# One ScalarE copy moved behind the second exponential in the attention stage of a fused two-block kernel

## The chip, the cores and the metric

The kernel runs on one core of a Trainium2 chip. A core has engines that run their own instruction queues and meet through semaphores: TensorE (PE, matrix products), VectorE (DVE), ScalarE (ACT), GpSimd (POOL) and SyncE (SP, which mostly issues DMAs). Products land in PSUM, eight banks of 512 fp32 columns on 128 partitions; ScalarE and VectorE read them from there. The metric is the device time of one execution in microseconds (us).

## The reference

The program computes two transformer-like blocks, one after the other, on 1024 tokens of width 1024. The first has differential attention, retention and a mixture of 32 experts, the second a gated convolution and an MLP. Only the differential attention matters here: four heads, each with two maps, causal in chunks of 64 tokens:

```python
s = jnp.einsum('bqhmd,bkhmd->bhmqk', q_blk, k) * scale
s = jnp.where(allowed, s + bias, -jnp.inf)
p = jax.nn.softmax(s, axis=-1)
a = p[:, :, 0] - lam * p[:, :, 1]
return jnp.einsum('bhqk,bkhe->bqhe', a.astype(v.dtype), v)
```

So every block of 128 queries needs the scores of two maps (m = 0 and 1), the softmax of each, their weighted difference, and the product with the values.

## The kernel before, in words

The kernel is written out by hand: each engine has one function with its instructions in order, and semaphores tie the functions together. No scheduler changes that order. The stages run one after the other: norm and transposes, the input projection (with retention in its middle), attention, output projection, router and experts, convolution, MLP.

The attention stage works on 32 blocks, numbered b. A block is one head h and one query tile i. Within each head the tiles come in the order 7, 0, 6, 1, 5, 2, 4, 3 (line 495), so that a large and a small block alternate. A block has i + 1 key tiles ("k tiles") of 128 columns, its width W is 128 times that. Even b are the large ones (8, 7, 6, 5 k tiles), odd b the small ones (1, 2, 3, 4). For each block:

- TensorE computes the scores of map m into SC(m), which is two PSUM banks of the tensor `ps` (lines 1815 to 1820). There is one such place for each map, so the scores of block b + 1 wait until the exponential of block b has read it (`att_exp`).
- VectorE takes the negated row maximum (line 1441, `att_max`).
- ScalarE takes the exponential with the row sum (line 1140, `att_exp`); the row sum leaves as a separate instruction, ACTIVATION_READ_ACCUMULATOR. The result goes to one of three buffers for each map, `PB`.
- VectorE, once both maps of the block have their sums, forms the reciprocals and the weighted difference (lines 1447 to 1453, `att_mixed`).
- TensorE transposes the difference, one k tile at a time, into two PSUM banks of `pt` (line 1830, `att_transposed`). There is a single place for this result.
- ScalarE copies the first four k tiles from there to SBUF (line 1122, `t_evac`, `att_t_act`), VectorE the k tiles above four, where there are any (line 1461, `late_evac`, `att_t_dve`). The next block's transposes wait for both.
- TensorE multiplies with the values (line 1844, `att_out`), and ScalarE reads the product twice, scaled and squared (lines 1127 and 1129, `o_evac`).

These steps are spread over several turns of the loop. In turn b TensorE issues: scores (b, 0), transposes (b - 2), scores (b, 1), output product (b - 3). VectorE issues: row maximum (b, 0), difference (b - 1), row maximum (b, 1), upper copy (b - 2). ScalarE issues: exponential (b, 0), copy (b - 2), exponential (b, 1), output readers (b - 3). The last turns, where no new scores exist, do what is left.

No DMA is issued inside the stage. GpSimd splits two weight units into halves at the stage's start (lines 982 and 984, up to 357 us).

Of the kernel before, what the change touches and what calls it, by code (L numbers as in the profile page):

```python
# [106 lines left out]
def build(nc, a, out):  # L107
    with ExitStack() as ctx:
# [122 lines left out]
        def tpair(par):  # L231
            return PT[:, 2 * par:2 * par + 2, :].rearrange("p b (k c) -> p (b k) c", k=4)
# [263 lines left out]
        NB = len(BLOCKS)  # L496

        def aT(par):
            return XTF[:, 6144 + par * 1024:6144 + (par + 1) * 1024].rearrange("p (k q) -> p k q", k=KT)

        def PB(b, m):
            i = 2 * (b % 3) + m
            return XTF[:, i * 1024:i * 1024 + 1024]

        def SC(m):
            return PS[:, 2 * m:2 * m + 2, :].rearrange("p b c -> p (b c)")
# [554 lines left out]
        def _(act):  # L1061
# [54 lines left out]
            def t_evac(b):  # L1116
                par = b % 2
                act.wait_ge(s_at, b + 1)
                if b >= 2:
                    act.wait_ge(s_ao, b - 1)  # L1120
                n = min(4, BLOCKS[b][1] + 1)
                nc.scalar.activation(aT(par)[:, 0:n, :], tpair(0)[:, 0:n, :], ACT.Copy).then_inc(s_aea, 1)

            def o_evac(b):
                h, i = BLOCKS[b]
                act.wait_ge(s_ao, b + 1)
                nc.scalar.activation(H[:, i, h * DV:(h + 1) * DV], PT[:, 2 + b % 2, 0:DV], ACT.Copy,
                                     scale=rows_rec[:, 2 * b:2 * b + 1])
                nc.scalar.activation(Z[:, b % 8 * DV:b % 8 * DV + DV], PT[:, 2 + b % 2, 0:DV],
                                     ACT.Square, scale=rows_rec[:, 2 * b:2 * b + 1],  # L1130
                                     accum_out=ssA[:, h * TT + i:h * TT + i + 1]).then_inc(s_aoe, 1)

            for b in range(NB + 3):
                if b < NB:
                    W = P * (BLOCKS[b][1] + 1)
                    for m in range(2):
                        act.wait_ge(s_amx, 2 * b + m + 1)
                        if b >= 3:
                            act.wait_ge(s_at, b - 2)
                        nc.scalar.activation(PB(b, m)[:, 0:W], SC(m)[:, 0:W], ACT.Exp,  # L1140
                                             bias=negmax[:, 2 * b + m:2 * b + m + 1],
                                             accum_out=rows_sum[:, 2 * b + m:2 * b + m + 1]).then_inc(s_ae, 1)
                        if m == 0 and b >= 2:
                            t_evac(b - 2)
                if NB <= b < NB + 2:
                    t_evac(b - 2)
                if b >= 3:
                    o_evac(b - 3)
# [1018 lines left out]
```

## Time and profile before

| | us |
|---|---|
| three executions | 2341.51, 2339.02, 2333.03 |
| median | 2339.02 |
| profiled execution, device time | 2341.51 |
| its span, first to last instruction | 2339.8 |
| TensorE busy | 2128.6 (91%) |
| VectorE busy | 1234.3 (53%) |
| ScalarE busy | 906.5 (39%) |
| GpSimd busy | 199.1 (9%) |

The attention lies between about 336 and 468 us of the span. From the second head on a head lasts 29.7 us: its first row maximum begins at 374.25, 403.99 and 433.74 us. A profile row in order of time gives the start, the duration, the engine, the line, what is written and read, and, in brackets, how long the engine stood idle before it and which instruction released it. Idle time counts only where the engine is on the path that sets the end. The granted clock is the share of full speed that TensorE's throttle allowed. Durations of neighbouring rows overlap where an engine is pipelined, so the distance of two starts says how long the engine is taken.

### The profile page before, as it was taken

The page shows a single profiled execution, that of the slowest core. Times are in us where ns is not written, and L with a number is a line of the kernel's source. Part 1 is how long each engine was busy: PE and PEld are TensorE (multiplying, and loading weights), DVE is VectorE, ACT ScalarE, POOL GpSimd, SP SyncE. Part 2 cuts the span into 40 slices and gives each one's busy share as a digit, 9 for nine tenths or more (in the row PEclk, how much of TensorE's full clock was granted, in tenths as well). Part 3 has the DMA queues.
Part 4 walks back from the last instruction along what each step waited for, and adds up shares of the span by engine and source line. Part 5 has one row for each costly group of instructions (what it writes and reads, how often), then busy time and mean ns, then how long its engine had stood idle before and what let it go on. Part 6 is the DMA issues. An engine that isn't in the chain of part 4 may idle for free.

```text
span 2339.8 us, 28085 instructions
## 1 busy us (share of the span) xinstructions
PE 2128.6 (91%) x10811; PEld 1091.7 (47%) x10811; DVE 1234.3 (53%) x1374; ACT 906.5 (39%) x1219; POOL 199.1 (9%) x264
## 2 busy tenths in 40 slices
PE   5998988888399999999945899959999999999999
PEld 3445446644244445445423465544444444444444
DVE  4225237744688888888867152384534343343432
ACT  4122126722267666666744152372312112211210
POOL 1000031000111111111120010022000000000000
PEclk9999999999699999999977899979999999999999
DMA  9101220051399999999975043325201011010001
GB/s 380 56 37 37 63 54 1 1 210 55 111 416 422 422 412 417 417 413 417 408 266 225 28 153 113 98 85 180 73 36 72 36 56 52 36 72 36 36 0 72
DMA packets 77020, 378.62 MB, mean 162 GB/s; under 512 B 12368, under 2 KB 19152, under 8 KB 44368
## 3 DMA queue, kind: packets, MB, share of 16 engines
q1 hardware_dynamic: 54000, 296.82, 32.1%
q0 software_dynamic: 22944, 80.75, 9.7%
q8 instruction: 52, 0.85, 0.2%
q14 instruction: 24, 0.20, 0.0%
HBM read 326.67 MB, written 37.75 MB: 156 GB/s over the span
## 4 chain that ended last, share of the span: by engine, by line
PE 86%; DVE 7%; issue 3%; DMA 2%; ACT 1%; SPq 1%; POOL 1%; POOLq 0%; DVEq 0%; ACTq 0%
PE ps L409 22%; PE ps L411 22%; PE ps L410 22%; PE pt L1954 5%; PE pt L409 1%; PE pt L410 1%; PE pt L411 1%; PE pt L1908 1%; DVE cols L1441 1%; PE pt L463 1%; PE pt L1844 1%; PE pt L2010 1%; PE pt L2012 1%; PE pt L2011 1%; DMA resid<-in_x 1%
## 5 line engine op out<-in xcount | busy, mean ns | idle before, releaser
L409 PE MATMUL ps<-xt,split 128*128 128x512 f16 x960 | 370.3, 386 | 22.8 <-issue 13.8
L409 PE MATMUL ps<-split,xt 128*128 128x512 f16 x928 | 354.5, 382 | 25.5 <-DMA xt<-arena 20.0
L410 PE MATMUL ps<-xt,split 128*128 128x512 f16 x960 | 369.7, 385 | 0.0
L411 PE MATMUL ps<-xt,split 128*128 128x512 f16 x960 | 369.4, 385 | 0.0
L411 PE MATMUL ps<-split,xt 128*128 128x512 f16 x928 | 354.4, 382 | 0.0
L410 PE MATMUL ps<-split,xt 128*128 128x512 f16 x928 | 354.3, 382 | 0.0
L546 DVE SCALAR_TENSOR_TENSOR split<-stage,split 128x2048 f16<-128x2048 f32 x128 | 290.1, 2287 | 57.8 <-ACT split L542 57.8
L542 ACT ACTIVATE split<-stage 128x2048 f16<-128x2048 f32 x128 | 237.1, 1901 | 121.1 <-PE ps L411 121.1
L411 PE MATMUL ps<-split,arena 128*128 128x512 f16 x512 | 194.3, 379 | 0.0
L410 PE MATMUL ps<-split,arena 128*128 128x512 f16 x512 | 194.3, 379 | 0.0
L409 PE MATMUL ps<-split,arena 128*128 128x512 f16 x512 | 194.3, 379 | 0.0
L1723 DVE SCALAR_TENSOR_TENSOR resid<-ps,resid 128x512 f32<-128x512 f32 x128 | 87.2, 690 | 191.7 <-PE ps L411 191.6
L409 PEld LDWEIGHTS ps<-xt,split 128*128 128x128 f16 x960 | 95.0, 99 | 139.0 <-issue 27.0
L1708 DVE TENSOR_TENSOR arena<-arena 128x512 f32<-128x512 f32 x64 | 44.3, 692 | 218.6 <-ACT arena L1322 218.6
L669 ACT ACTIVATE split<-stage 128x2048 f16<-128x2048 f32 x32 | 59.4, 1900 | 252.9 <-PE ps L411 252.9
L409 PEld LDWEIGHTS ps<-split,xt 128*128 128x128 f16 x928 | 91.3, 98 | 135.8 <-issue 35.2
L411 PEld LDWEIGHTS ps<-xt,split 128*128 128x128 f16 x960 | 95.2, 99 | 117.2 <-issue 6.9
L410 PEld LDWEIGHTS ps<-xt,split 128*128 128x128 f16 x960 | 95.1, 99 | 114.7 <-issue 5.5
L410 PEld LDWEIGHTS ps<-split,xt 128*128 128x128 f16 x928 | 91.2, 98 | 112.5 <-issue 12.5
L411 PEld LDWEIGHTS ps<-split,xt 128*128 128x128 f16 x928 | 91.2, 98 | 111.0 <-issue 2.7
L1322 ACT ACTIVATE arena<-ps 128x512 f32<-128x512 f32 x64 | 38.2, 597 | 244.1 <-PE ps L411 244.1
L1954 PE MATMUL pt<-arena,xt 128*128 128x512 f32 x256 | 115.1, 593 | 0.0
(291 smaller groups left out, 3010.3 us busy)
## 6 DMA issues: line engine op xcount, KB each, us to landing
stage<-in_w_gate SPq DMA_DIRECT2D x64, 1024.0 KB, 7.9
stage<-in_w_up SPq DMA_DIRECT2D x64, 1024.0 KB, 8.0
arena<-in_w_down SPq DMA_DIRECT2D x64, 1024.0 KB, 9.9
stage<-in_w_mlp SPq DMA_DIRECT2D x32, 1024.0 KB, 5.3
y_rows<-arena POOLq DMA_DIRECT2D x48, 512.0 KB, 8.7
arena<-in_conv_taps POOLq DMA_DIRECT2D x32, 576.0 KB, 4.3
stage<-in_w_dense_a SPq DMA_DIRECT2D x16, 1024.0 KB, 8.9
stage<-in_w_dense_b SPq DMA_DIRECT2D x12, 1024.0 KB, 9.0
```

Of the source, the lines that this page charges most:

```text
L409: nc.tensor.matmul(out_ap, lh, rh, start=start, stop=False)
L410: nc.tensor.matmul(out_ap, lh, rl, start=False, stop=False)
L411: return nc.tensor.matmul(out_ap, ll, rh, start=False, stop=stop)
L463: i = nc.tensor.transpose(tpair(t % 2)[:, k, :], src(t, k), ident)
L542: nc.scalar.activation(whi(s), wstage(s), ACT.Copy, scale=WS).then_inc(s_wh[s], 1)
L546: nc.vector.scalar_tensor_tensor(out=wlo(s), in0=wstage(s), scalar=WS, in1=whi(s), op0=ALU.mult, op1=ALU.subtract).then_inc(s_wo[s], 1)
L669: nc.scalar.activation(whi(s), wstage(s), ACT.Copy, scale=WS).then_inc(s_wh[s], 1)
L1322: nc.scalar.activation(relu[j % 2], PS[:, j % 4, :], ACT.Relu, scale=IWS)\
L1441: nc.vector.tensor_reduce(negmax[:, 2 * b + m:2 * b + m + 1], SC(m)[:, 0:W], AX.X, ALU.max, negate=True).then_inc(s_amx, 1)
L1708: nc.vector.tensor_tensor(relu2[j % 2], relu[j % 2], relu[j % 2], ALU.mult).then_inc(s_relu, 1)
L1723: nc.vector.scalar_tensor_tensor(out=H[:, t, hs], in0=PS[:, j % 4, :], scalar=IWS, in1=H[:, t, hs], op0=ALU.mult, op1=ALU.add).then_inc(s_ ...
L1954: m = nc.tensor.matmul(PT[:, 3, :], hTf[:, k, :], native(q)[:, k * UC:k * UC + UC], start=k == 0, stop=k == UK - 1)
```

## The change

In ScalarE's loop the copy of block b - 2 stands between the two exponentials of block b before the change. After it, the copy stands behind both, ahead of the output readers of block b - 3. The copy, its waits and its signal are the same, and so are all other instructions. In the last turns (b = 32, 33) nothing changes place.

```diff
@@ -1140,9 +1140,7 @@
                         nc.scalar.activation(PB(b, m)[:, 0:W], SC(m)[:, 0:W], ACT.Exp,
                                              bias=negmax[:, 2 * b + m:2 * b + m + 1],
                                              accum_out=rows_sum[:, 2 * b + m:2 * b + m + 1]).then_inc(s_ae, 1)
-                        if m == 0 and b >= 2:
-                            t_evac(b - 2)
-                if NB <= b < NB + 2:
+                if 2 <= b < NB + 2:
                     t_evac(b - 2)
                 if b >= 3:
                     o_evac(b - 3)
```

Place one, ScalarE at the start of a head (turns b = 24 and 25, the large block with 8 k tiles and the small one with 1). Before, `L1140` is the exponential, `L1122` the copy, `L1127` and `L1129` the output readers; `att_transposed` is given by the transposes, `att_max` by the row maximum:

```order
L1140 ACTIVATE xt,cols<-ps,cols 128x1024 [waits att_transposed,att_max]
L1122 ACTIVATE xt<-pt 128x512 [waits att_out,att_transposed]
L1140 ACTIVATE xt,cols<-ps,cols 128x1024 [waits att_transposed,att_max]
L1127 ACTIVATE resid<-pt,cols 128x128 [waits att_out]
L1129 ACTIVATE zone,cols<-pt,cols 128x128
L1140 ACTIVATE xt,cols<-ps,cols 128x128 [waits att_transposed,att_max]
L1122 ACTIVATE xt<-pt 128x512 [waits att_out,att_transposed]
L1140 ACTIVATE xt,cols<-ps,cols 128x128 [waits att_transposed,att_max]
```

The same place in the changed kernel, where x2 are the two exponentials in a row:

```order
L1140 ACTIVATE xt,cols<-ps,cols 128x1024 [waits att_transposed,att_max] x2
L1122 ACTIVATE xt<-pt 128x512 [waits att_out,att_transposed]
L1127 ACTIVATE resid<-pt,cols 128x128 [waits att_out]
L1129 ACTIVATE zone,cols<-pt,cols 128x128
L1140 ACTIVATE xt,cols<-ps,cols 128x128 [waits att_transposed,att_max] x2
L1122 ACTIVATE xt<-pt 128x512 [waits att_out,att_transposed]
```

The copy of block 22 has moved behind the second exponential of block 24, and the copy of block 23 behind the second exponential of block 25.

Place two, TensorE at the turn that follows (turn 25 begins with the first row; this order is the same before and after). `L1815` to `L1820` are scores, `L1830` transposes, `L1844` the output product; `att_t_act` is given by ScalarE's copy, `att_t_dve` by VectorE's:

```order
L1815 MATMUL ps<-arena 128x128 [waits att_exp]
L1816 MATMUL ps<-xn,arena 128x128
L1817 MATMUL ps<-zone 128x128
L1820 MATMUL ps<-half 128x128
L1830 MATMUL pt<-misc,xt 128x128 [waits att_t_dve,att_t_act,att_mixed]
L1830 MATMUL pt<-misc,xt 128x128 x3
L1815 MATMUL ps<-arena 128x128 [waits att_exp]
```

Nothing moved here: the transposes of block 23 wait for the copy of block 22, and the second scores of block 25 stand behind them.

Place three, ScalarE at the end of the stage (turn b = 31 and what follows). Before:

```order
L1140 ACTIVATE xt,cols<-ps,cols 128x512 [waits att_transposed,att_max]
L1122 ACTIVATE xt<-pt 128x384 [waits att_out,att_transposed]
L1140 ACTIVATE xt,cols<-ps,cols 128x512 [waits att_transposed,att_max]
L1127 ACTIVATE resid<-pt,cols 128x128 [waits att_out]
L1129 ACTIVATE zone,cols<-pt,cols 128x128
```

And in the changed kernel:

```order
L1140 ACTIVATE xt,cols<-ps,cols 128x512 [waits att_transposed,att_max] x2
L1122 ACTIVATE xt<-pt 128x384 [waits att_out,att_transposed]
L1127 ACTIVATE resid<-pt,cols 128x128 [waits att_out]
L1129 ACTIVATE zone,cols<-pt,cols 128x128
```

The last copy that moves is that of block 29; those of blocks 30 and 31 stand where they stood.

## Rows read from the trace of the kernel before

**Rows 1.** The page: the chain that ended last, by engine.
```profile
PE 86%; DVE 7%; issue 3%; DMA 2%; ACT 1%; SPq 1%; POOL 1%; POOLq 0%; DVEq 0%; ACTq 0%
```

**Rows 2.** Stretches: busy us (x instructions) of PE, PEld, DVE, ACT, POOL; clock, DMA.
```profile
404.00:433.70 29.70, 26.68 (x198) 19.53 (x197) 22.42 (x44) 20.97 (x64) 0.00 (x0) 1.00 0.00 1
```

**Rows 3.** Waits from 353 to 462 us: who waited for whom, us, times, longest.
```profile
ACT xt L1140 <- DVE cols L1441: 36.3, 44, 4.3
...
DVE cols L1441 <- PE ps L1820: 19.2, 17, 1.7
DVE cols L1447 <- ACT xt L1140: 3.6, 7, 0.9
...
PE pt L1830 <- DVE xt L1461: 10.9, 15, 2.4
```

**Rows 4.** Order in time, ScalarE: start us, duration us, instruction, turn 24.
```profile
436.11 0.59 ACT L1122 ACTIVATE xt<-pt 128x512 f32<-128x512 f32 x1
437.30 1.11 ACT L1140 ACTIVATE xt<-ps,cols 128x1024 f32<-128x1024 f32 x1 [0.61 <-DVE cols L1441]
438.31 0.19 ACT L1140 ACTIVATION_READ_ACCUMULATOR xt<-ps,cols 128x1 f32 x1
438.41 0.36 ACT L1127 ACTIVATE resid<-pt,cols 128x128 f32<-128x128 f32 x1
```

**Rows 5.** Order in time, TensorE, turns 25 and 26.
```profile
437.61 0.63 PE L1830 MATMUL pt<-misc,xt 128*128 128x128 f32 x4 [0.95 <-DVE xt L1461]
438.56 0.23 PE L1815 MATMUL ps<-arena 128*128 128x128 f16 x1 [0.32 <-ACT xt L1140]
...
439.97 0.38 PE L1815 MATMUL ps<-arena 128*128 128x512 f16 x1
...
441.16 1.04 PE L1830 MATMUL pt<-misc,xt 128*128 128x128 f32 x8
442.04 0.38 PE L1815 MATMUL ps<-arena 128*128 128x512 f16 x1
```

**Rows 6.** Order in time, ScalarE turn 18 (7 k tiles), TensorE turn 19.
```profile
414.81 1.01 ACT L1140 ACTIVATE xt<-ps,cols 128x896 f32<-128x896 f32 x1 [0.49 <-DVE cols L1441]
...
415.52 0.30 PE L1830 MATMUL pt<-misc,xt 128*128 128x128 f32 x1 [0.54 <-DVE xt L1461]
415.96 0.28 PE L1815 MATMUL ps<-arena 128*128 128x256 f16 x1
```

**Rows 7.** Order in time, ScalarE turn 20 (6 k tiles), TensorE turn 21.
```profile
422.22 0.90 ACT L1140 ACTIVATE xt<-ps,cols 128x768 f32<-128x768 f32 x1 [0.33 <-DVE cols L1441]
...
422.80 0.41 PE L1830 MATMUL pt<-misc,xt 128*128 128x128 f32 x2 [0.61 <-DVE xt L1461]
423.27 0.34 PE L1815 MATMUL ps<-arena 128*128 128x384 f16 x1
```

**Rows 8.** Order in time, turns 22 (5 k tiles) and 23, three engines.
```profile
429.14 0.79 ACT L1140 ACTIVATE xt<-ps,cols 128x640 f32<-128x640 f32 x1 [0.40 <-DVE cols L1441]
...
429.58 0.52 PE L1830 MATMUL pt<-misc,xt 128*128 128x128 f32 x3 [0.38 <-DVE xt L1461]
430.08 0.39 PE L1815 MATMUL ps<-arena 128*128 128x512 f16 x1
...
431.37 0.68 DVE L1441 TENSOR_REDUCE cols<-ps 128x1 f32<-128x512 f32 x1
```

**Rows 9.** Order in time, VectorE, turns 25 and 26.
```profile
440.25 0.28 DVE L1441 TENSOR_REDUCE cols<-ps 128x1 f32<-128x128 f32 x1
441.36 1.09 DVE L1441 TENSOR_REDUCE cols<-ps 128x1 f32<-128x896 f32 x1 [0.82 <-PE ps L1820]
```

**Rows 10.** Stretches of TensorE alone: busy us (x), granted clock, DMA.
```profile
350.75:353.19 2.44, 0.00 (x0) 0.91 0.00 0
353.19:359.69 6.50, 6.50 (x28) 0.51 0.00 0
415.52:419.23 3.71, 3.57 (x29) 1.00 0.00 0
```

## The prediction, made before the changed kernel ran

> **What bounds the kernel now.** I read four views in this order. The page's chain of waits first: TensorE carries 86% of it, so time spent elsewhere counts only where TensorE stands still for it [rows 1]. Then the busy times of one head of the attention, the only stage that the change touches: in 29.7 us TensorE is busy 26.7, VectorE 22.4 and ScalarE 21.0 [rows 2]. ScalarE, whose order changes, is the least loaded of the three. Then the waits of the stage: ScalarE waits 44 times, 36.3 us in all, and always for VectorE's row maximum; VectorE waits 17 times, 19.2 us, for TensorE's scores; TensorE waits 15 times, 10.9 us, and that before the transposes, for the copy of the upper k tiles on VectorE (line 1461) [rows 3]. Last the order in time around such a wait.
>
> Names: S(b,m) are the score products of block b and map m, R(b,m) its row maximum (VectorE), E(b,m) its exponential (ScalarE), X(b) the transposes, T(b) ScalarE's copy of the first four k tiles out of PSUM, L(b) VectorE's copy of the others, A(b) the output products, O(b) their two readers on ScalarE. In step b TensorE runs S(b,0), X(b-2), S(b,1), A(b-3).
>
> **What the change takes away.** T(b-2) no longer stands ahead of E(b,1). It is 0.59 us for 512 columns. At each place shown it had ended before E(b,1) could begin: T(22) runs from 436.11 to 436.70 and E(24,1) then still waits 0.61 us for R(24,1), up to 437.30 [rows 4]. Of the 44 waits in rows 3, 30 stand before second maps, one before each from b = 2 on; the smallest at the places priced below is 0.33 us, at the third. So E(b,1) begins when it did, and the gain of the moved copy is 0. All of T was cover for a wait that remains.
>
> **What it adds.** X(b-1), one step later, writes the PSUM banks that T(b-2) reads and so waits for T(b-2) and L(b-2). Before, T was done long ahead and L, which starts right behind R(b,1), ended the wait. Now T starts only when E(b,1) is through, and E(b,1) itself starts after R(b,1). L is at most as long as T, so T is the later one wherever X is reached early. That is in every second step, where S(b+1,0) belongs to a small block (1 to 4 k tiles) and is over soon. In the other steps X comes behind the scores of five to eight k tiles, and the copy (behind a short exponential) is ready.
>
> Two lags are read off. The next ScalarE instruction starts where the duration of an exponential ends (437.30 + 1.11 = 438.41), and TensorE starts 0.06 us after the accumulator read behind an exponential ends (438.31 + 0.19 = 438.50, start at 438.56) [rows 4, 5]. Thus X can start at E's start + E's duration + 0.59 + 0.06. Eight transposes take from 441.16 to 442.04, 0.11 each [rows 5]. S(b+1,1) follows X, and had waited until then for E(b,1) [rows 5], so only the part of the delay beyond that wait is a loss:
> - Place 1, after 8 k tiles: X at 438.41 + 0.65 = 439.06 where it was at 437.61; four transposes, S at 439.52 where it was at 438.56: 0.96 us [rows 4, 5].
> - Place 2, after 7 tiles: X at 414.81 + 1.01 + 0.65 = 416.47 (was 415.52), one transpose, S at 416.58 (was 415.96): 0.62 [rows 6].
> - Place 3, after 6 tiles: 422.22 + 0.90 + 0.65 = 423.77 (was 422.80), two, S at 423.99 (was 423.27): 0.72 [rows 7].
> - Place 4, after 5 tiles: 429.14 + 0.79 + 0.65 = 430.58 (was 429.58), three, S at 430.91 (was 430.08): 0.83 [rows 8].
>
> Does that reach the end? At place 1 S(25,1) ends near 439.52 + 0.42 = 439.94, while R(25,1) begins only at 440.25, because VectorE is in the subtraction of block 24 [rows 9]: the second map of the small block loses nothing. But A(22) stands directly behind S(25,1) in TensorE's queue, S(26,0) directly behind A(22), and R(26,0) begins at 441.36 when TensorE, not VectorE, is ready (0.82 us of wait) [rows 5, 9]. So the loss goes through TensorE's own queue into the next large block, and from there into everything. It is the same at the other three: VectorE's 17 waits in rows 3 stand there. Queued behind the later T on ScalarE are O(b-3) and E(b+1,0), both by at most 0.5 us; E(25,0) started at about 438.41 + 0.6, now at 439.5, and is over by 440.0, while S(26,0), which waits for it, starts only at 439.97 + 0.96 [rows 5]. No term from that. DMA: none is issued in the stage.
>
> Sum over four heads. Place 1 exists three times (it needs the head before): 2.9. Place 2 four times: 2.5; in the first head VectorE is slow there, and I take the same. Place 3 four times: 2.9. Place 4 three times: 2.5, and at the last one there is no next large block; what remains is the last E, 0.45 us later (S ends at 430.91 + 0.91 = 431.82 where R began at 431.37) [rows 8]: 0.5. Together **11.3 us**.
>
> **The clock.** At place 1 TensorE now stands still from 436.66 to 439.06, 2.40 us, where it was 0.95 [rows 5]. The trace has one such gap in this stage, 2.44 us, and the granted clock fell from full (2.4 GHz) to half (1.2 GHz) inside it (mean 0.91) and stayed there for the 6.5 us that followed. The same work (one transpose, scores, eight output tiles, scores) took 3.71 us later at full clock: 2.8 us lost [rows 10]. Bounds for each of the three gaps at place 1: 0 and 2.8. At the other places the gap is 1.4 to 1.6 us, for which no row shows a fall; I take 0. I take one fall of the three and, as a part of it may end earlier or lie on slack, 2.0 us. [...]
>
> Forecast: 11.3 + 2.0 = **13.3 us longer**. The profiled execution took 2341.51 us (span 2339.8); it would take 2354.8. That execution is the slowest of three, 2.5 above the median of 2339.02, so for a median I say **2352.3 us**.
>
> **Rivals**
> - A, the copies come late, no clock fall: 2339.0 + 11.3 = 2350.3. For it: the clock is at full in the whole head of rows 2. Against: the gap of rows 10.
> - B, a fall at all three gaps: 2339.0 + 11.3 + 8.4 = 2358.7. For it: each gap is as long as the one that fell. Against: that one came soon after another low stretch.
> - C, half is absorbed: the step behind a loss has waits of its own (VectorE before the subtraction 7 times, 3.6 us in all [rows 3]), and each place gives back about half: 2344.7. Against: the queue TensorE, R, TensorE has no such wait at the four places.
> - D, nothing: X is in fact held by L and the accumulator, and the copy comes no later than L: 2339. It needs R(b,1) to end over 1.4 us ahead of what the rows show.
> - E, faster: the waits of E(b,1) are put down to R but are partly T's. Then each of the 30 exponentials behind a copy starts up to 0.5 us earlier, the subtraction and S(b+1,1) with it. In the 15 large steps this would be up to 7 us: 2332. It decides from the point where T ends after R(b,1). Rows 4 and 6 to 8 show R ending 0.3 to 0.6 us after it, so I give it little.
>
> **How the numbers follow.** Forecast 0.42, A 0.26, B 0.15, C 0.08, D 0.05, E 0.04. No change means within 0.5%, which is 11.7 us, about what a measurement of this kernel can tell. The border lies inside my cases: of the forecast four fifths lie above it, of A two fifths, B all. Slower 0.34 + 0.10 + 0.15 = 0.59; faster 0.04; the same 0.37. Range: from C's 2344 to 2361, B with the 2.5 us by which medians differ. The likeliest one's own is 2349 to 2356.
>
> **What the profile will show.** If right: the wait of TensorE before the transposes is put down to ScalarE's copy (line 1122, which moves up two lines), about 15 times and some 25 us in all; heads last 32.5 to 33 us where they lasted 29.7, or 35 with a fall; ScalarE's waits for R keep their places; work after the attention is as long as before. Wrong: if transposes still wait for line 1461, if a head lasts under 31 us, or if TensorE's granted clock is below full at every head. If E(b,1) starts earlier against R(b,0) than before, case E holds.

## The result and the profile after

The changed kernel took 2352.27 us (median of 6 runs, 2349.26 to 2354.6), the kernel before 2337.23 us (median of 6, 2333.03 to 2341.51). The ratio is 1.006 with a 95% interval of 1.0048 to 1.0073, that is 11 to 17 us: slower, clear of noise, though the lower end of the interval lies just under the 0.5% that I had called the border. The medians are 15.0 us apart; 13.3 was predicted.

The profiled execution took 2348.84 us (span 2347.1), where 2354.8 was forecast; that is 7.3 more than that of before. The two profiles differ outside the stage too, by 5.9 us in the other direction: ScalarE's first exponential begins 2.5 us earlier (337.75 against 340.22), and what follows the stage is 3.5 us shorter (1868.7 against 1872.15). Nothing was changed there, and the six runs of the kernel before spread by 8.5 us. So I judge by the stage itself, from ScalarE's first exponential to the table load behind the attention. It lasted 127.4 us before (340.22 to 467.65) and 140.6 after: 13.2 more.

The ends of the stage after, in order of time on ScalarE (start, duration, line):

```profile
337.75 1.11 ACT L1140 ACTIVATE xt<-ps,cols 128x1024 f32<-128x1024 f32 x1
...
478.40 1.28 ACT L1148 ACT_TABLE_LOAD   x1
```

Lines below the change have moved up by two: the transposes are now 1828, VectorE's row maximum 1439, its copy 1459. ScalarE's copy stands above the change and is still line 1122. The waits of the stage after (353 to 477 us; us in all, times, longest):

```profile
ACT xt L1140 <- DVE cols L1439: 44.3, 43, 4.0
DVE cols L1439 <- PE ps L1818: 31.2, 22, 2.8
...
PE pt L1828 <- ACT xt L1122: 24.0, 14, 2.4
```

Against [rows 3]: the transposes wait for ScalarE's copy where they waited for VectorE's, 24.0 us instead of 10.9, and no wait for VectorE's copy is left. That the 13.1 us between them are so near to the 13.2 that the stage grew is chance: over the whole stage the two are 26.5 and 11.8, the short waits before the second scores (0.32 us at 438.56 in [rows 5]) are gone, and a fall of the clock, below, is no wait. VectorE's wait for the scores grew by 12.0: the delay handed on.

The same place as [rows 4, 5, 9], in turns 24 to 26 after, engine by engine in order of time:

```profile
444.81 1.11 ACT L1140 ACTIVATE xt<-ps,cols 128x1024 f32<-128x1024 f32 x1 [1.10 <-DVE cols L1439]
445.91 0.59 ACT L1122 ACTIVATE xt<-pt 128x512 f32<-128x512 f32 x1
...
446.60 0.63 PE L1828 MATMUL pt<-misc,xt 128*128 128x128 f32 x4 [2.44 <-ACT xt L1122]
447.06 0.22 PE L1813 MATMUL ps<-arena 128*128 128x128 f16 x1
...
448.46 0.38 PE L1813 MATMUL ps<-arena 128*128 128x512 f16 x1
...
449.85 1.09 DVE L1439 TENSOR_REDUCE cols<-ps 128x1 f32<-128x896 f32 x1 [1.81 <-PE ps L1818]
```

The second exponential now waits 1.10 us for the row maximum, 0.61 + 0.49: the copy's whole place has turned into waiting. The copy ends at 446.50, the transposes start at 446.60, and the scores of the next large block (448.46) stand 1.40 us behind the second scores (447.06) of the small one, as before (438.56 to 439.97, 1.41).

The heads, from the first exponential of the large block to that of the next head (columns: length, busy time and count of TensorE, its weight loads, DVE, ACT and POOL, then the granted clock and the DMA's):

```profile
375.06:408.10 33.04, 26.06 (x198) 19.75 (x197) 22.61 (x45) 21.22 (x65) 0.00 (x0) 1.00 0.01 1
408.10:442.50 34.40, 27.42 (x198) 21.05 (x197) 22.70 (x45) 21.32 (x64) 0.00 (x0) 0.95 0.00 1
```

A head was 29.7 us [rows 2]. One head is now at full clock and 3.30 us longer, one has a fall of the clock and is 4.65 us longer. The gap at place 1 is 2.44 us in the second, the third and the fourth head alike, and the clock is not: it fell through that of the third head (the first two rows) and not through that of the fourth (TensorE alone: busy, granted clock):

```profile
409.75:412.19 2.44, 0.00 (x1) 0.89 0.00 0
412.19:416.09 3.90, 3.90 (x22) 0.63 0.00 0
444.16:446.60 2.44, 0.00 (x1) 1.00 0.01 3
446.60:450.50 3.90, 3.90 (x33) 1.00 0.02 4
```

In the same 3.90 us TensorE began 22 instructions at the lower clock and 33 at the full one.

### The profile page after: what moved, and what is told of

It is laid out like the page before. It is cut to its first block, busy times and chain, and to the rows that moved or that the text cites. A ratio compares the mean times of both kernels' runs of the same rounds, so it can differ in the third digit from the quotient of the medians.

```text
span 2347.1 us, 28085 instructions
## 1 busy us (share of the span) xinstructions
PE 2123.1 (90%) x10811; PEld 1092.8 (47%) x10811; DVE 1235.2 (53%) x1374; ACT 908.0 (39%) x1219; POOL 199.7 (9%) x264
## 4 chain that ended last, share of the span: by engine, by line
PE 84%; DVE 6%; issue 3%; SPq 3%; DMA 2%; ACT 1%; POOL 0%; POOLq 0%; ACTq 0%; DVEq 0%
PE ps L409 22%; PE ps L410 22%; PE ps L411 22%; PE pt L1952 5%; SPq L637 2%; PE pt L1906 1%; PE pt L409 1%; PE pt L411 1%; PE pt L410 1%; DVE cols L1439 1%; PE pt L463 1%; PE pt L1842 1%; PE pt L2008 1%; PE pt L2009 1%; PE pt L2010 1%
```

## The experiments

Each is measured by its heads (29.7 us before, 33.0 after at full clock) and its stage (127.4 and 140.6). First heads vary by a microsecond or two between executions, with the low clock at the stage's start, so a single stage length is good to about that; heads two and three repeat to 0.02 us where the clock is the same. Where a kernel has one timed execution, no ratio is given. The time in a head in which TensorE is not busy (its length less TensorE's busy time) is a second measure: it leaves out what a fall of the clock costs. In the changed kernel it is 33.04 - 26.06 = 6.98 us, at full clock and, within 0.01, with a fall.

**The copy between the exponentials in even turns alone.**

```diff
-                        if m == 0 and b >= 2:
+                        if m == 0 and b >= 2 and b % 2 == 0:
                             t_evac(b - 2)
-                if NB <= b < NB + 2:
+                if NB <= b < NB + 2 or (2 <= b < NB and not (b % 2 == 0)):
```

> The copy goes back between the two exponentials in the even turns (large blocks) alone; in odd turns it stays behind. Stage length is counted from ScalarE's first exponential to the table load behind the stage: 127.4 us before, 140.6 after the change. Theory (the loss is the copy of an even turn coming late for the transposes of the next, small turn): stage 127.4 +- 0.5, time as before, no wait of line 1830 for line 1122. Rival (any copy behind the second exponential costs, since it pushes the output readers and the next exponential back by 0.5 us): about half of the loss stays, stage near 134.

Measured: 2338.45 us against 2337.59, ratio 1.0008 (0.9997 to 1.0019); stage 128.8, heads 30.21. The loss is nearly gone, and no wait of the transposes is put down to ScalarE's copy. But the heads are 0.47 us longer than before, which neither side had, and the stage is 1.3 us longer, outside the 0.5 allowed. The place is the next large turn (ScalarE, then TensorE, in order of time):

```profile
439.98 0.59 ACT L1122 ACTIVATE xt<-pt 128x512 f32<-128x512 f32 x1
...
440.67 1.06 PE L1830 MATMUL pt<-misc,xt 128*128 128x128 f32 x8 [0.29 <-issue]
```

The transposes of the large block start 0.10 us behind the copy's end (440.57). They could have started at 439.02 + 1.19 = 440.21, behind their own turn's scores (439.02 is the start of those scores, 1.19 the distance from scores to transposes before, 439.97 to 441.16 [rows 5]). The profile gives no releaser for this gap, but it ends with the copy. So an odd copy that is late does cost, 0.46 us once a head; in the changed kernel TensorE arrives there 0.96 us later anyway, and this term is hidden.

**The complement: between them in odd turns alone.** The condition is `b % 2 == 1`.

> The complement: the copy is between the exponentials in odd turns (small blocks) and behind them in even turns. Theory: the whole loss is here, stage 138.7 to 141 depending on the clock, time 12 to 15 us above before. Rival (half the loss from each parity): stage near 134, time +7.

Measured: 2353.04 us, ratio 1.007 (1.0054 to 1.0087), stage 142.0. The wait is the changed kernel's, 26.0 us in 15 times. The heads are 34.68 and 34.67 us, each with a fall of the clock (mean 0.95). TensorE is not busy for 34.68 - 27.71 = 6.97 us of a head, as in the changed kernel (6.98). So all of the loss lies with the even turns' copies; the rival that gives each parity half is out. The stage is 1 us above the expected 138.7 to 141: the clock fell in all three heads where I had allowed for fewer falls.

**Behind only in turns 8, 16 and 24, and behind only in the other even turns.** The conditions for standing between are `b % 8 != 0` and `b % 2 == 1 or b % 8 == 0`.

> The copy is behind only in turns 8, 16 and 24 (the first turn of heads two to four), the three places with a 2.4 us gap on TensorE. Theory: 3 x 0.96 = 2.9 us plus 1.4 to 2.8 for each fall of the clock; stage 130.3 without a fall, 132 to 133 with one. Rival (the clock is most of the loss, and it falls through these gaps): stage 136 or more.

> The copy is behind in even turns 2, 4, 6, 10, 12, 14, 18, 20, 22, 26, 28 and 30, and between in all others. Theory: 4 x 0.62 + 4 x 0.72 + 3 x 0.83 + 0.5 = 8.4 us, no fall of the clock after the first head; stage 135.8. Rival (the clock is most of the loss): stage under 131.

Measured: the heads of the first are 32.37 and 30.73 us (stage 132.0, time 2341.87), those of the second 32.05 and 32.04 (stage 136.0, time 2349.47):

```profile
373.04:405.41 32.37, 28.20 (x198) 0.95 0.01 1
405.41:436.14 30.73, 26.55 (x198) 1.00 0.00 1
```

```profile
378.64:410.69 32.05, 26.24 (x198) 1.00 0.00 1
```

Both are what the theory says (expected: stage 132 to 133 with one fall, and 135.8). Place 1 without a fall is 30.73 - 29.74 = 0.99 us (predicted 0.96), places 2 to 4 together 2.30 (predicted 2.17), and 0.99 + 2.30 makes the 3.30 of the changed kernel. A fall through the place 1 gap costs 32.37 - 30.73 = 1.64 us. In the second kernel no clock falls after the first head.

**The copy cut short, in both kernels.** Only one k tile is copied by ScalarE; the others are left out, as the expectations say.

```diff
-                nc.scalar.activation(aT(par)[:, 0:n, :], tpair(0)[:, 0:n, :], ACT.Copy).then_inc(s_aea, 1)
+                nc.scalar.activation(aT(par)[:, 0:1, :], tpair(0)[:, 0:1, :], ACT.Copy).then_inc(s_aea, 1)
```

> The changed kernel, its copy on ScalarE cut to one k tile (128 columns, 0.28 us instead of 0.59; the other k tiles are left uncopied, so the product with the values is of old data there). Theory (transposes start when the copy ends): each of the 15 places with a copy of 3 or 4 k tiles gains 0.3 us, stage 136 to 136.5 without a fall of the clock, one to three us more with one. Rival (what costs is the order, that is the second exponential ahead of the copy, not the copy's length): stage unchanged at 140.6.

> The kernel before, its copy on ScalarE cut to one k tile (the others left uncopied). Theory (between the exponentials the copy is hidden in the wait for the row maximum): stage 127.4 +- 0.4. Rival (part of ScalarE's waits ahead of the second exponential belongs to the copy, case E of the prediction): stage 3 to 7 us shorter.

Measured: in the changed kernel the heads go to 31.76 us at full clock, 1.28 less for four copies a head that are each 0.31 shorter (4 x 0.31 = 1.24); stage 135.9 with one fall later on. The gain of each copy is as expected; the 136 to 136.5 expected without a fall was a wrong sum, since the 140.6 that it starts from holds a fall already. In the kernel before nothing moves, 29.74 us (its stage of 126.1, below the expected 127 to 127.8, is shorter in the first head alone):

```profile
376.71:408.47 31.76, 26.06 (x198) 1.00 0.01 1
```

```profile
372.41:402.15 29.74, 26.72 (x198) 1.00 0.01 1
```

So the 0.31 us cut off are on the path in full behind the exponential, and not at all between the exponentials. Case E of the prediction is out.

**The copy behind the output readers too.**

```diff
-                if 2 <= b < NB + 2:
-                    t_evac(b - 2)
-                if b >= 3:
+                if b >= 3 and b < NB:
                     o_evac(b - 3)
+                if 2 <= b < NB + 2:
+                    t_evac(b - 2)
+                if b >= NB:
+                    o_evac(b - 3)
```

> The changed kernel with the copy moved once more, behind the two output readers (0.59 us) of the same turn. Theory: transposes start later by the readers' 0.59 us at the 16 places, stage 140.6 + 9 = about 149 to 150, more if the longer gaps let the clock fall. Rival (the transposes are held by something that ends at the same time, so that a further delay is partly hidden): stage under 145.

Measured: stage 164.0, heads 40.76 us, time 2374.46. The direction was right and the size was not: 23 us instead of 9. Two things were left out. The smaller one: in the odd turns the readers have a wait of their own, for the output product, which TensorE issues after the second scores, and the copy queued behind them inherits it (ScalarE, one odd turn):

```profile
426.26 0.37 ACT L1127 ACTIVATE resid<-pt,cols 128x128 f32<-128x128 f32 x1 [1.40 <-PE pt L1844]
...
426.87 0.60 ACT L1122 ACTIVATE xt<-pt 128x512 f32<-128x512 f32 x1
```

The larger one is the clock. The gap at place 1 grew to 3.05 us, and from the second head on the clock falls at three of the four places of each head (gaps of 3.05, 2.1 and 2.4 us; mean clock 0.87):

```profile
377.72:418.48 40.76, 31.16 (x197) 23.98 (x196) 22.94 (x45) 21.33 (x64) 0.00 (x0) 0.87 0.00 1
```

Against the changed kernel's head of 33.04 us this one is 7.72 longer. TensorE is not busy for 9.60 us instead of 6.98, which is 2.62 more, where the readers alone would give 4 x 0.59 = 2.36; and it is busy for 31.16 us instead of 26.06 with the same work, 5.10 more, which is what three falls cost.

**The place 1 gaps of the changed kernel filled with work.**

```diff
             for b in range(NB + 3):
                 if b < NB:
                     att_scores(b, 0)
+                if b % 8 == 1 and 8 < b < NB:
+                    pe.wait_ge(s_aoe, b - 4)
+                    for _ in range(11):
+                        nc.tensor.matmul(PT[:, 2 + (b - 3) % 2, DV:512], QQ[0][:, 0, 0:P], KK[0][:, 0, 0:512 - DV],
+                                         start=True, stop=True)
```

> The changed kernel with 11 extra products of 384 columns (0.16 us each, 1.8 us) at turns 9, 17 and 25, between the first scores and the transposes, into PSUM columns that nothing reads: they fill most of the 2.4 us gaps and nothing waits for them. Theory: no fall of the clock after the first head, stage 138.7 +- 0.5 (the two or so us of the clock gone, the 11.3 of the late copy left). Rival (extra work in the gap delays the transposes, or the clock did not cost): stage 140.6 or more.

Measured: stage 138.5, heads 33.03 and 33.03 us at full clock, time 2348.09. The extra products fit into the gap, and the transposes start behind the copy as before:

```profile
443.22 1.95 PE L1852 MATMUL pt<-arena 128*128 128x384 f16 x11
445.82 0.63 PE L1828 MATMUL pt<-misc,xt 128*128 128x128 f32 x4 [0.65 <-issue]
```

So the clock term is real: without the fall the third head is 1.37 us shorter (34.40 to 33.03), and the two kernels are equal to 0.01 us where neither has one. Of the 2.1 us between the stages the other 0.75 lies in the first head, where nothing was filled. That the filling is what kept the clock up rests on this one execution: two of the three unfilled gaps of the changed kernel brought no fall either.

**The output product ahead of the second scores, in the kernel before.** The rows of before show TensorE idle between the transposes of a small turn and its second scores, which wait for the exponential of the large block [rows 5]. The output product can stand there.

```diff
                 if 2 <= b < NB + 2:
                     att_transposes(b - 2)
+                early = b % 2 == 1 and 3 <= b < NB
+                if early:
+                    att_out(b - 3)
                 if b < NB:
                     att_scores(b, 1)
-                if b >= 3:
+                if b >= 3 and not early:
                     att_out(b - 3)
```

> The kernel before with one change on TensorE: in odd turns the output product of block b-3 stands ahead of the second scores instead of behind them, so that it fills the time in which those scores wait for the exponential. Theory (that wait, not the copies, bounds each small turn of the kernel before; ahead of it TensorE stands idle): the next large block's scores start 0.5, 0.3, 0.2 and 0.2 us earlier at places 1 to 4, heads 28.5 us instead of 29.7, time 4 to 5 us below before (ratio 0.998). Rival (the second scores come later by the product's 0.9 to 1.8 us, and their row maximum and exponential bound the next turn): heads as long as before or longer, time +0 to +5.

Measured over 11 runs: 2332.69 us against 2335.7, ratio 0.9984 (0.9974 to 0.9994); heads 28.50 us, stage 122.9.

```profile
371.61:400.11 28.50, 26.03 (x198) 1.00 0.01 1
```

The heads are what was worked out. The time fell by 3.0 us (interval 1.4 to 6.1) where 4 to 5 was expected; the fourth head and the tail took 32.44 us against 32.65, so little of the gain came there. It is the fastest of all kernels tried, by a little.

**The same on the changed kernel.**

> The changed kernel with the same reordering on TensorE. Theory (transposes wait for the late copy, and behind them the same work stands in TensorE's queue in either order, with no wait left to fill): heads 33.0 us as in the changed kernel without a fall of the clock. Rival (the loss came through the second scores' lateness): heads 31.8 or less.

Measured: heads 36.22 (with a fall) and 34.97 us (full clock), stage 151.1, time 2368.52. A miss by 1.9 us a head. The second scores come later here, behind the transposes, the copy's wait and the output product; with them come the second exponential of the small turn and the copy behind it, and then the large block's transposes find that copy late. Row one is ScalarE's copy, row two TensorE's transposes behind it, from this kernel:

```profile
447.90 0.48 ACT L1122 ACTIVATE xt<-pt 128x384 f32<-128x384 f32 x1
...
448.48 0.73 PE L1828 MATMUL pt<-misc,xt 128*128 128x128 f32 x5 [0.67 <-issue]
```

To test that, the copies of the odd turns went back between the exponentials:

> As e10 (changed kernel, output product ahead of the second scores in odd turns), but with the copies of odd turns back between the exponentials. e10's heads were 35.0 us without a fall of the clock where 33.0 was expected. Theory for that miss: the second scores come later, so do the second exponential of the odd turn and the copy queued behind it, and now the large block's transposes wait for that copy as well. Then here heads return to 33.0 to 33.3 us without a fall (1.5 more with one). Rival (the second scores' lateness itself bounds the next turn, whatever the copy does): heads stay near 35.

Measured: heads 34.51 and 34.32 us, each with a fall of the clock (mean 0.95), stage 142.4, time 2352.88. A head without a fall was not seen, but TensorE's idle time does not depend on it (the heads of this kernel, TensorE alone):

```profile
373.60:408.11 34.51, 27.55 (x198) 0.95 0.00 1
408.11:442.43 34.32, 27.36 (x198) 0.95 0.00 1
```

TensorE is not busy for 6.96 us in either head, as in the changed kernel (6.98), where it was 34.97 - 26.36 = 8.61 us with the odd copies behind. So the odd turn's late copy was the cause of the miss.

## Why the prediction was right

- **Removing the copy from between the exponentials gives nothing.** Right. ScalarE's wait before the second exponential grew by the copy's place (0.61 to 1.10 us), and cutting the copy there by 0.31 us changed no head by more than 0.01 us.
- **The transposes of small turns wait for the copy.** Right: 14 waits, 24.0 us in the window shown, 15 and 26.5 us in the whole stage, where 15 and some 25 were expected. One premise was misread: VectorE's copy of 512 columns takes 0.68 us, longer than ScalarE's 0.59, so L is not "at most as long as T". It does no harm, as T begins later by a whole exponential (0.79 to 1.11 us). The copy's line did not move up by two either.
- **Only what exceeds the exponential's own wait is lost, four places.** Right: 0.99 and 2.30 us against 0.96 and 2.17, 3.30 a head against 3.13. The missing 0.17 is the start lag: transposes follow the copy's end by about 0.10 us, not by the 0.06 read off an accumulator read, four times a head.
- **The loss goes through TensorE's queue to the next large block.** Right: its scores follow the small turn's second scores by 1.40 us in either kernel. Of VectorE's 17 waits, though, 14 stand ahead of a large block's first row maximum; the other three, of 0.2 us, stand ahead of a second one.
- **The other turns cost nothing.** Right for this kernel, for a reason the prediction gave only half of. The odd copies are late too, by 0.46 us once a head; only because TensorE is later still does it not show.
- **One fall of the clock, 2.0 us.** The count was right, the size a little high: one of three gaps, 1.36 us in that head (1.64 where place 1 alone was moved). The count was a choice between none and three, and other kernels with the same gaps had one or three, so it is luck. The rows of before had given 2.8 us, with a mean clock of 0.51 over 6.50 us [rows 10]; behind the new gap the low stretch was shorter, a mean of 0.63 over 3.90 us. The prediction also says that the trace had one such gap; it has three of 2.3 to 2.5 us at the stage's start, and behind the first (2.53 us, up to 341.48) the clock fell 1.0 us later too.
- **The end.** The fourth head and the tail grew by 3.25 us where 2.8 was expected; the start lag makes up 0.2 of that.
- **The sum.** 2.0 + 3.3 + 4.65 + 3.25 = 13.2 us of stage by the profile, 13.3 predicted. The closeness owes something to errors that cancel: the places were priced low by about 0.2 a head, the clock high by 0.6, the first head at 2.2 where 2.0 came. The first head's 2.0 is no measurement of the places: the same instructions took 37.31 us there in the changed kernel and 36.56 in the one with filled gaps. The timed difference of 15.0 agrees within its interval of 11 to 17. That the median came out at 2352.27 us, with 2352.3 forecast, is luck too: the median of before, from which I had added, was 2339.02 for three runs and 2337.23 for six.

Case A (no fall) and case B (three) stood beside the forecast as rivals. Case B's state exists: the kernel with copies between in odd turns had falls at all three place 1 gaps. Case A's was seen only with the gaps filled. Which gap of 2.44 us brings a fall was not controlled. Cases C and D are out: a head at full clock lost 3.30 us, all that the four places add up to, and no transposes wait for VectorE's copy.

## What to carry to other kernels

An instruction that stands ahead of a wait in an in-order queue can be free there, and on the path one place later: before moving it behind, read who waits for its result and how long the wait ahead of it was. Price each place as the delay of the result less the slack that the next consumer had for another reason, and follow the queue of the consumer to the next instruction that has no slack. Two delays on the same path need not add: the odd turns' copies cost 0.47 us a head alone and nothing beside the even ones.

## What the runs showed of the hardware

A wait of TensorE for a ScalarE copy out of PSUM can cost it the clock. Four kernels have the full copy behind the exponential at place 1 and nothing in the gap: the changed one, the one with odd turns between, the one with turns 8, 16 and 24 alone, and the last one above. There twelve gaps of 2.4 us preceded eight falls (1, 3, 1 and 3 of three); two equal gaps in one execution went different ways. Shorter gaps did it too: at place 1 the kernel with the short copy (2.12 us) had one fall in three, and the changed kernel with the output product early (2.14 us) two in three. Gaps of 1.4 to 1.6 us (nine in the fourth experiment's kernel behind the first head) brought none. The Trainium skill, "TensorE: Matmul & The Clock Gate", section "Loop structure matters more than you think", says of a loop whose next products follow immediately that a copy out of PSUM does not break the clock. Here the next products had to wait for the copy, so the page's case is another one, and no run here tests it.

The separate read of the accumulator is shown as 0.19 to 0.22 us, but ScalarE's next instruction starts 0.10 us behind its start, just where the exponential's own duration ends. A plain copy lets its successor in about 0.1 us ahead of its own end. So a row sum costs the queue some 0.2 us less than the sum of the rows suggests.
